# Attention heads of an mLSTM layer: scores of two heads issued together, in three PSUM phases

## The chip, the cores and the metric

One NeuronCore of one Trainium2 chip runs one inference step of a two-layer trunk in float32. The metric is the device time of one execution in microseconds (us), the median over runs. Everything below is about a single core, so no core waits for another.

## What is computed

The trunk has two layers. Layer 0 mixes tokens with an mLSTM (8 heads, keys of 64, values of 128), layer 1 with an S5 state-space model; each is followed by a squared-ReLU MLP. There are 512 prompt tokens in one sequence and 8 sample sequences of 8 tokens, so 576 columns in all. What the change touches is the mLSTM of layer 0, and the final RMSNorm. Cut to that:

```python
for each head h (q, k of width 64, v of width 128, gates i and f):
    logD[t, s] = b[t] - b[s] + li[s]          # s <= t, b is the cumulative sum of log f
    m_t  = max(b[t] + m0, max_s logD[t, s])   # running stabiliser
    s    = (q @ k.T) * 64**-0.5 * exp(logD - m_t)
    num  = exp(b + m0 - m_t) * (q @ C0) + s @ v
    den  = exp(b + m0 - m_t) * (q @ n0) + sum(s)
    h_t  = num / max(|den|, exp(-m_t))
    C1   = decay * C0 + sum_s ws * k v        # new matrix state, and n1 alike
out = (h * rsqrt(mean(h*h) + eps) * head_g * sigmoid(o)) @ w_out
...
y = x * rsqrt(mean(x*x) + eps) * g            # final norm
```

## The kernel before

Activations lie as features by tokens: 128 partitions by 576 columns. Large products are made by `product` (L384) as three products of halves of split float32 numbers. Before the attention stage stands the projection into q, k, v, o; behind it the output projection (`product` with `I_OUT`, weights brought by `load_slab`), then the MLP.

Each engine runs its own list, in program order, and semaphores tie the lists together. In the attention stage each of the lists of TensorE, VectorE, ScalarE and GpSimd has a loop `for h in range(H + 1)` in which work of head h and of head h-1 is interleaved by hand. For head h:

- SyncE sends a row of u to all partitions (`load_u_row`, L510), two buffers, and the matrix state of the sample sequences (`load_state`, L527); it stores the new state (L542, L546) after `c_new`.
- ScalarE makes `exps(h)` (L1017), the decay weights of 512 + 384 + 256 + 128 columns, into `E[:, h % 2]`.
- TensorE makes `scores(h)` (L1910, L1912): q and k of one head lie on 64 partitions, heads 2i on partitions 0 to 63 and heads 2i+1 on 64 to 127. The result fills PSUM banks 1 to 3.
- VectorE multiplies scores and exponentials in `weights(h)` (L1449 over 1280 columns, L1450 for the samples), which signals `p_done`; GpSimd zeroes the upper triangle in `mask(h)` (L745) and signals `p_masked`.
- TensorE makes `sums(h)`: ten products of weights and values (L1935), one of the samples (L1936), and four with the old state `Cst` (L1940), then `pv_done`. The first three sums lie in bank 4, the rest in bank 5.
- ScalarE copies the sums out (L1042, L1043) and scales the state part into `Is` (L1044), signalling `ot_act`. VectorE adds it in (L1526, `ot_ready`).
- TensorE's `updates_b(h)` (L1946, L1963) waits for `ot_act`, since it writes bank 4; `updates_a(h)` follows after the next scores. GpSimd's `keys(h)` (L777 to L781) prepares both, and `sample_queries(h)` (L763) the products with `Cst`.
- VectorE runs `states_b` (L1470 on), `head_norm` (L1497 to L1503), `states_a` (L1456, `c_new`), `normed` (L1508, L1509, `htok_ready`); between them ScalarE makes the squares (L1033) and GpSimd a power (L796).
- TensorE transposes the normed head in `heads_out` (L1921, L1922); VectorE gates it (L1479, L1480), ScalarE casts it (L1022), VectorE makes the low half `hid_lo` (L1485).

TensorE's order in step h is: `updates_b(h-1)`, `scores(h+1)`, `updates_a(h-1)`, `sums(h)`, `heads_out(h-1)`. `weights(h+1)` reads the three banks that `scores(h+2)` will write, so `scores` waits for `p_done`.

Ahead of the loop TensorE transposes keys and values (L1896, L1897), makes the argument of the samples' exponent (L1968), and `scores(0)`; ScalarE makes the samples' exponent (L1025) and then `exps(0)`; GpSimd masks it (L756).

At the very end the sums of squares for the final norm are made by 27 products with `ones` (L2210), over `acc`, `tbuf` and `R`, the last of which needs the last square.

## Time and profile before

| | us |
|---|---|
| median of 3 runs | 1359.15 |
| lowest and highest | 1357.31, 1359.29 |
| profiled execution | 1361.22 |
| its span | 1359.5 |
| TensorE busy | 1306.1 (96%) |
| VectorE busy | 789.5 (58%) |
| ScalarE busy | 491.0 (36%) |
| GpSimd busy | 356.1 (26%) |

The mean granted clock of TensorE is 0.977 of full speed. The attention stage lies between about 201 and 297 us of the span. Times in the rows are microseconds from the start of the span; PE is TensorE's matmul, PEld its weight load, DVE VectorE, ACT ScalarE, POOL GpSimd, SPq SyncE's DMA queue. A float32 product shows as two instructions, a transpose as one.

### The profile page before, as it was taken

How to read it: one execution, taken by the hardware profiler on the slowest of the kernel's cores; microseconds unless marked ns; L12 is line 12 of the kernel's file. 1: busy time of each engine (PE TensorE's matmuls, PEld its weight loads, DVE VectorE, ACT ScalarE, POOL GpSimd, SP SyncE). 2: the span in 40 equal slices, each digit the busy share in tenths (PEclk: the TensorE clock that was granted, in tenths of full speed). 3: DMA queues.
4: the chain of work that ended last, by engine and by line, in shares of the span. 5: the costliest groups of instructions: out<-in, count | busy, mean ns of one | idle time of the engine just before them, and what ended most of it. 6: DMA issues, size and time to landing. Idle time of an engine off the chain costs nothing.

```text
span 1359.5 us, 24599 instructions
## 1 busy us (share of the span) xinstructions
PE 1306.1 (96%) x9929; PEld 1264.0 (93%) x9929; DVE 789.5 (58%) x1102; ACT 491.0 (36%) x743; POOL 356.1 (26%) x360
## 2 busy tenths in 40 slices
PE   4999998999999999999999889999999999999997
PEld 3999996789999999999999878999999999999997
DVE  6662334766783583343345557334588586686785
ACT  5311133543341341341341224423453452543553
POOL 3000004535799990000018553022000000000001
PEclk9999997999999999999999877999999999999999
DMA  5232231324323223223224995233223313223222
GB/s 149 63 91 81 77 95 45 90 59 89 90 78 93 78 77 93 77 81 88 77 78 127 161 133 135 75 91 106 80 77 94 93 62 104 82 94 94 80 75 70
DMA packets 223039, 121.81 MB, mean 90 GB/s; under 512 B 34752, under 2 KB 218744, under 8 KB 222976
## 3 DMA queue, kind: packets, MB, share of 16 engines
q1 hardware_dynamic: 222144, 120.74, 34.7%
q8 instruction: 42, 0.69, 0.2%
q10 hardware_dynamic: 832, 0.21, 0.1%
q14 instruction: 21, 0.17, 0.0%
HBM read 110.18 MB, written 10.75 MB: 89 GB/s over the span
## 4 chain that ended last, share of the span: by engine, by line
PE 84%; DVE 8%; SPq 2%; ACT 2%; issue 2%; DMA 1%; POOL 0%; ACTq 0%; DVEq 0%; POOLq 0%
PE ps L384 62%; PE ps L2131 12%; PE ps L1935 2%; DVE wlo L368 2%; PE ps L1910 1%; PE ps L2087 1%; PE ps L2083 1%; SPq L645 1%; DMA late<-d_taps 1%; SPq L626 1%; PE ps L1946 1%; PE ps L1940 1%; DVE R L405 1%; PE ps L1963 1%; DVE x L1634 1%
## 5 line engine op out<-in xcount | busy, mean ns | idle before, releaser
L384 PE MATMUL ps<-xg_hi,whi 128*128 128x288 f32 x1424 | 305.8, 296 | 3.2 <-DVE wlo L368 1.7
L384 PE MATMUL ps<-xg_hi,wlo 128*128 128x288 f32 x1424 | 304.4, 295 | 0.0
L384 PE MATMUL ps<-xg_lo,whi 128*128 128x288 f32 x1424 | 303.1, 294 | 0.0
L363 ACT ACTIVATE whi<-raw 128x1024 fp32r<-128x1024 f32 x115 | 121.5, 1058 | 352.7 <-PE ps L384 336.0
L384 PEld LDWEIGHTS ps<-xg_hi,whi 128*128 128x128 f32 x1424 | 228.2, 188 | 5.6 <-issue 2.3
L384 PEld LDWEIGHTS ps<-xg_lo,whi 128*128 128x128 f32 x1424 | 228.0, 188 | 0.0
L384 PEld LDWEIGHTS ps<-xg_hi,wlo 128*128 128x128 f32 x1424 | 227.5, 188 | 0.0
L368 DVE TENSOR_TENSOR wlo<-raw,whi 128x1024 fp32r<-128x1024 f32 x115 | 170.9, 1486 | 76.0 <-ACT whi L363 75.9
L384 PE MATMUL ps<-hid_hi,whi 128*128 128x288 f32 x896 | 192.4, 296 | 2.4 <-DVE hid_lo L1779 2.1
L384 PE MATMUL ps<-hid_lo,whi 128*128 128x288 f32 x896 | 192.2, 296 | 0.0
L384 PE MATMUL ps<-hid_hi,wlo 128*128 128x288 f32 x896 | 191.5, 294 | 0.0
L384 PEld LDWEIGHTS ps<-hid_hi,whi 128*128 128x128 f32 x896 | 143.6, 189 | 3.9 <-DVE hid_lo L1779 2.8
L384 PEld LDWEIGHTS ps<-hid_hi,wlo 128*128 128x128 f32 x896 | 144.0, 189 | 0.0
L384 PEld LDWEIGHTS ps<-hid_lo,whi 128*128 128x128 f32 x896 | 143.6, 188 | 0.0
L1535 DVE TENSOR_TENSOR x<-x,ps 128x576 f32 (+1 forms) x40 | 30.2, 754 | 124.9 <-PE ps L384 124.9
L925 POOL TENSOR_TENSOR acc<-hB 128x576 f32<-128x576 f32 x1 | 1.8, 1774 | 350.8 <-ACT hB L1156 350.8
L2131 PE MATMUL ps<-hB_hi,whi 128*128 128x288 f32 x256 | 76.0, 297 | 0.6 <-DVE x L1634 0.6
L2131 PE MATMUL ps<-hB_hi,wlo 128*128 128x288 f32 x256 | 75.4, 295 | 0.0
L2131 PE MATMUL ps<-hB_lo,whi 128*128 128x288 f32 x256 | 75.4, 294 | 0.0
L1553 DVE TENSOR_TENSOR tbuf<-rbuf,R 128x576 f32<-128x576 f32 x32 | 35.7, 1116 | 68.1 <-ACT rbuf L1060 68.0
L1634 DVE TENSOR_TENSOR x<-x,ps 128x288 f32<-128x288 f32 x112 | 50.3, 451 | 32.4 <-PE ps L2131 31.9
L1327 DVE TENSOR_TENSOR qkvo<-ps,R 128x576 f32 (+1 forms) x25 | 18.9, 756 | 77.4 <-PE ps L384 77.3
(397 smaller groups left out, 2083.3 us busy)
## 6 DMA issues: line engine op xcount, KB each, us to landing
raw<-in_ffn_w_up SPq DMA_DIRECT2D x64, 512.0 KB, 4.0
raw<-in_ffn_w_down SPq DMA_DIRECT2D x32, 512.0 KB, 4.2
raw<-in_ffn_w_down SPq DMA_DIRECT2D x16, 1024.0 KB, 5.2
raw<-in_mlstm_w_in SPq DMA_DIRECT2D x25, 512.0 KB, 3.8
raw<-in_s_w_glu SPq DMA_DIRECT2D x16, 512.0 KB, 3.9
raw<-in_mlstm_w_out SPq DMA_DIRECT2D x8, 512.0 KB, 4.2
late<-d_taps SPq DMA_DIRECT2D x32, 128.0 KB, 8.0
d_u<-unat SPq DMA_DIRECT2D x8, 288.0 KB, 2.4
```

Of the source, the lines that this page charges most:

```text
L363: nc.scalar.activation(whi[:, s], raw[:, s], ACT.Copy).then_inc(whi_done, 1)
L368: nc.vector.tensor_tensor(wlo[:, s], raw[:, s], whi[:, s].bitcast(F32), ALU.subtract).then_inc(w_ready, 1)
L384: last = nc.tensor.matmul(ps[:, 2 * s + c, 0:HN], w[:, s, k, :], a[:, k, c * HN:(c + 1) * HN], start=(k == 0 and n == 0), stop=(k == KT - ...
L405: nc.vector.reciprocal(R[:], R[:]).then_inc(R_ready, 1)
L626: sp.dma_start(U2[i * GC:(i + 1) * GC, g, :], d_u.rearrange("(g c) t b -> t c g b", c=GC)[T - 1 - i, :, g]).then_inc(u2_in[half], 16)
L645: sp.dma_start(taps_pair[j][i * GC:(i + 1) * GC], d_taps[2 * j * P:(2 * j + 2) * P, i * GC:i * GC + P].rearrange("(g c) m -> c g m", c=GC) ...
L1327: V.tensor_tensor(halves(tile(qkvo, t)), slab_ps(s), halves(R[:]), ALU.mult).then_inc(ps_free[s], 1)
L1535: V.tensor_tensor(halves(tile(x, m)), halves(tile(x, m)), slab_ps(s), ALU.add).then_inc(ps_free[s], 1)
L1553: V.tensor_tensor(tbuf[:], rbuf[:], R[:], ALU.mult).then_inc(scaled, 1)
L1634: V.tensor_tensor(xh, xh, ps[:, bank, 0:HN], op).then_inc(x_added, 1)
L1935: nc.tensor.matmul(o, e[:, c:c + P], Vtok[:, 1 + j, h, :], start=(j == 0), stop=(j == i))
L2131: last = nc.tensor.matmul(out, w[wi][:, k, :], hi[:, k, t, :], start=(first and k == 0 and n == 0), stop=(k == 3 and n == 2), skip_group_c ...
```

## The change

- Scores are made for a pair of heads (2i, 2i+1) in three phases: banks 0 and 1 take the first 512 columns of both heads, banks 2 and 3 the next 512 (384 + 128), and the last 256 and the samples go to banks 0 and 1 again (banks 6 and 7 for the first pair). Within a phase the products alternate between the two heads, so between partitions 0 to 63 and 64 to 127. Phases 1 and 2 of the next pair are issued in each odd step, phase 3 within `sums`.
- `weights` becomes three instructions, `weights_1`, `_2`, `_3`, of 512, 512 and 256 columns. `weights_1` of both heads of a pair stands ahead of `states_a` in odd steps.
- `E` gets a third buffer; ScalarE makes exponentials two heads ahead. `exps(0)` goes ahead of the samples' exponent, `exps(1)` behind it.
- `keys(0)` goes ahead of the mask of the samples' exponent; in the loop `keys` goes ahead of `mask` and waits for `updates_a` where it waited for `updates_b`; `mask(0)` goes ahead of `sample_queries(0)`.
- After three of the four prompt sums TensorE signals `pv3_done`; ScalarE copies them then (`ot3_act`), and `updates_b` waits for that copy alone.
- `heads_out(h-1)` moves from behind `sums(h)` into it, ahead of the four products with `Cst`.
- 24 transposes of `ident` into bank 5, whose result nobody reads, follow the first pair's scores.
- SyncE sends rows of u for heads 2 and 3 before the loop, and that of head h+4 between the store and the load of the state.
- The final sums run over `acc` first, then `tbuf`, then `R`, each over all columns, with the waits in front of each.

```diff
@@ -208,8 +208,8 @@
-        E = qkvo[:, 16 - KT:16, :].rearrange("p a n -> p (a n)")[:, 0:2688].rearrange("p (s n) -> p s n", s=2)
-        Es = qkvo[0:TS, 16 - KT:16, :].rearrange("p a n -> p (a n)")[:, 2688:2688 + H * TS]
+        E = qkvo[:, 16 - KT:16, :].rearrange("p a n -> p (a n)")[:, 0:4032].rearrange("p (s n) -> p s n", s=3)
+        Es = qkvo[0:TS, 16 - KT:16, :].rearrange("p a n -> p (a n)")[:, 4032:4032 + H * TS]
...
@@ -529,18 +529,20 @@
 
             load_state(0)
             load_state(1)
+            load_u_row(2)
+            load_u_row(3)
             sp.wait_ge(m_ready, 1)
             with nc.allow_non_contiguous_dma(reason="72 numbers"):
                 sp.dma_start(s_m[0].rearrange("b h -> h b"), gs[:, MPT:MPT + B]).then_inc(out_done, 16)
                 sp.dma_start(p_m[0].rearrange("b h -> h b"), gs[:, MPT + B:MPT + B + 1]).then_inc(out_done, 16)
             for h in range(H):
                 s = h % 2
-                if h + 2 < H:
-                    load_u_row(h + 2)
                 sp.wait_ge(c_new, h + 1)
                 for b2 in range(2):
                     sp.dma_start(s_C[0, b2::2, h].rearrange("b d e -> d b e"),
                                  Cst[b2 * DK:(b2 + 1) * DK, s, :, 0:DV]).then_inc(c_out[s], 16)
+                if h + 4 < H:
+                    load_u_row(h + 4)
                 if h + 2 < H:
                     load_state(h + 2)
                 sp.dma_start(p_C[0, 0, h], CP[:, s, :]).then_inc(c_out[s], 16)
...
@@ -751,11 +753,30 @@
+            def keys(h):
+
+                s = h % 2
+                if h >= 2:
+                    pool.wait_ge(upa_done, h - 1)
+                kc = slice(h % 2 * DK, (h % 2 + 1) * DK)
+                own.link(nc.gpsimd.tensor_tensor(Kws[0:TS, s, 0, :], Ktok[0:TS, 0, h // 2, kc],
+                                                 EX[0:TS, 0, h:h + 1].to_broadcast([TS, DK]), ALU.mult))
+                own.link(nc.gpsimd.tensor_tensor(Kws[:, s, 1:5, :], Ktok[:, 1:5, h // 2, kc],
+                                                 EX[:, 1:5, h:h + 1].to_broadcast([P, NB, DK]), ALU.mult))
+                nc.gpsimd.tensor_tensor(Kblk[:, s], Kws[0:TS, s, 0, :].unsqueeze(1).to_broadcast([TS, B, DK]),
+                                        MB[:].unsqueeze(2).to_broadcast([TS, B, DK]), ALU.mult).then_inc(kws_ready, 1)
+
+            pool.wait_ge(ex_ready, 2)
+            own.link(nc.gpsimd.tensor_scalar(EX[:, :, 0:H], EX[:, :, 0:H], DK ** -0.5, None, ALU.mult))
+            pool.wait_ge(kv_act, 6)
+            pool.wait_ge(kv_dve, 6)
+            keys(0)
             pool.wait_ge(us_exp, 1)
             es = Es.rearrange("s (h t) -> s h t", h=H)
             nc.gpsimd.tensor_tensor(es, es, Msk[:].unsqueeze(1).to_broadcast([TS, H, TS]), ALU.mult).then_inc(es_ready, 1)
             def sample_queries(h):
 
+                pool.wait_ge(p_masked, h + 1)
                 if h:
                     pool.wait_ge(pv_done, h)
                 hp = h % 2 * DK
@@ -768,35 +789,17 @@
                 last.then_inc(qblk_ready, 1)
                 pool.wait_ge(qblk_ready, h + 1)
 
...
-            def keys(h):
-
-                s = h % 2
-                if h >= 2:
-                    pool.wait_ge(upb_done, h - 1)
...
-            pool.wait_ge(ex_ready, 2)
-            own.link(nc.gpsimd.tensor_scalar(EX[:, :, 0:H], EX[:, :, 0:H], DK ** -0.5, None, ALU.mult))
-            pool.wait_ge(kv_act, 6)
-            pool.wait_ge(kv_dve, 6)
-            keys(0)
+
+            mask(0)
             sample_queries(0)
             n_column(0)
-            mask(0)
             for h in range(H + 1):
                 if h:
                     pool.wait_ge(ms_ready, h)
                     nc.gpsimd.tensor_tensor(st5[:, 5, :], st5[:, 4, :], st5[:, 6, :], ALU.pow).then_inc(rstd_ready, 1)
                 if h + 1 < H:
+                    keys(h + 1)
                     mask(h + 1)
-                    keys(h + 1)
                     sample_queries(h + 1)
                     n_column(h + 1)
             square_sums(pool, 1)
...
@@ -1008,10 +1011,10 @@
 
             def exps(h):
 
-                e = E[:, h % 2]
+                e = E[:, h % 3]
                 act.wait_ge(ub_in[h % 2], 16 * (h // 2 + 1))
-                if h >= 2:
-                    act.wait_ge(pv_done, h - 1)
+                if h >= 3:
+                    act.wait_ge(pv_done, h - 2)
                 for j in range(NB):
                     w = L - j * P
                     last = nc.scalar.activation(e[:, OFF[j]:OFF[j] + w], Ub[h % 2][:, j * P:L], ACT.Exp, bias=TK[:, 1 + j, h:h + 1])
@@ -1021,9 +1024,11 @@
                 act.wait_ge(hf_ready, h + 1)
                 nc.scalar.activation(hid_hi[:, h], qkvo[:, 16 + h], ACT.Copy).then_inc(hhi_done, 1)
 
+            act.wait_ge(kv_done, 12)
+            exps(0)
             act.wait_ge(us_arg, 2)
             nc.scalar.activation(Es, Es, ACT.Exp).then_inc(us_exp, 1)
-            exps(0)
+            exps(1)
             for h in range(H + 1):
                 if h:
                     act.wait_ge(ot_ready, h)
@@ -1032,14 +1037,16 @@
                     for i in range(5):
                         last = nc.scalar.activation(Htok[:, i, :], OT[:, i, 0:DV], ACT.Square, accum_out=st5[:, 2, i:i + 1])
                     last.then_inc(ssq_done, 1)
-                if h + 1 < H:
-                    exps(h + 1)
+                if h + 2 < H:
+                    exps(h + 2)
                 if h < H:
 
-                    act.wait_ge(pv_done, h + 1)
+                    act.wait_ge(pv3_done, h + 1)
                     if h:
                         act.wait_ge(htok_ready, h)
-                    nc.scalar.activation(OT[:, 1:4, :], ps[:, 4, 0:3 * E1].rearrange("p (i c) -> p i c", i=3), ACT.Copy)
+                    nc.scalar.activation(OT[:, 1:4, :], ps[:, 4, 0:3 * E1].rearrange("p (i c) -> p i c", i=3),
+                                         ACT.Copy).then_inc(ot3_act, 1)
+                    act.wait_ge(pv_done, h + 1)
                     nc.scalar.activation(OT[:, 4, :], ps[:, 5, 0:E1], ACT.Copy)
                     nc.scalar.activation(Is[:], ps[0:TS, 5, 2 * E1:3 * E1], ACT.Copy, scale=EX[0:TS, 0, 64 + h:65 + h]).then_inc(ot_act, 1)
                 if h:
...
@@ -1440,14 +1447,26 @@
             dve.wait_ge(att_const, 1)
             own.link(V.memset(st5[:, 6, :], -0.5))
 
-            def weights(h):
-
-                e = E[:, h % 2]
+            def weights_1(h):
+
                 dve.wait_ge(exp_done, h + 1)
-                dve.wait_ge(s_done, h + 1)
-                flat = ps[:].rearrange("p b c -> p (b c)")
-                V.scalar_tensor_tensor(e[:, 0:1280], flat[:, 512:1792], DK ** -0.5, e[:, 0:1280], ALU.mult, ALU.mult)
-                V.scalar_tensor_tensor(e[0:TS, 1280:1344], flat[0:TS, 1792:1856], DK ** -0.5, Es[:, h * TS:(h + 1) * TS],
+                dve.wait_ge(s_done, h // 2 * 3 + 1)
+                e = E[:, h % 3, 0:512]
+                V.scalar_tensor_tensor(e, ps[:, h % 2, :], DK ** -0.5, e, ALU.mult, ALU.mult).then_inc(p1_done, 1)
+
+            def weights_2(h):
+
+                dve.wait_ge(s_done, h // 2 * 3 + 2)
+                e = E[:, h % 3, 512:1024]
+                V.scalar_tensor_tensor(e, ps[:, 2 + h % 2, :], DK ** -0.5, e, ALU.mult, ALU.mult)
+
+            def weights_3(h):
+
+                dve.wait_ge(s_done, h // 2 * 3 + 3)
+                e = E[:, h % 3]
+                b = h % 2 + (6 if h < 2 else 0)
+                V.scalar_tensor_tensor(e[:, 1024:1280], ps[:, b, 0:256], DK ** -0.5, e[:, 1024:1280], ALU.mult, ALU.mult)
+                V.scalar_tensor_tensor(e[0:TS, 1280:1344], ps[0:TS, b, 256:320], DK ** -0.5, Es[:, h * TS:(h + 1) * TS],
                                        ALU.mult, ALU.mult).then_inc(p_done, 1)
...
@@ -1490,8 +1509,11 @@
                             TK[0:TS, 0, 0:H].unsqueeze(2).to_broadcast([TS, H, TS]), ALU.add).then_inc(us_arg, 1)
             dve.wait_ge(us_arg, 1)
             V.tensor_scalar(Es, Es, 0.0, None, ALU.min).then_inc(us_arg, 1)
+            weights_1(0)
+            weights_2(0)
             dve.wait_ge(es_ready, 1)
-            weights(0)
+            weights_3(0)
+            weights_1(1)
             def head_norm(h):
 
                 own.link(V.scalar_tensor_tensor(st5[:, 0, :], OT[:, :, DV], -1.0, OT[:, :, DV], ALU.mult, ALU.max))
@@ -1514,11 +1536,15 @@
                 if h:
                     states_b(h - 1)
                     head_norm(h - 1)
+                if h % 2 and h + 1 < H:
+                    weights_1(h + 1)
+                    weights_1(h + 2)
+                if h:
                     states_a(h - 1)
-                if h:
                     normed(h - 1)
                 if h + 1 < H:
-                    weights(h + 1)
+                    weights_2(h + 1)
+                    weights_3(h + 1)
                 if h:
                     gated(h - 1)
                 if h < H:
@@ -1899,17 +1925,27 @@
             pe.wait_ge(kv_dve, 6)
             pe.wait_ge(att_const, 2)
 
-            def scores(h):
-
-                if h:
-                    pe.wait_ge(p_done, h)
-                hp = h % 2 * DK
-                q, k = qkvo[hp:hp + DK, h // 2], qkvo[hp:hp + DK, 4 + h // 2]
-                for j, (b, c) in enumerate(((1, 0), (2, 0), (3, 0), (2, 384))):
+            def scores(i, phase):
+
+                if phase == 1 and i:
+                    pe.wait_ge(p_done, 2 * i)
+                elif phase == 3 and i:
+                    pe.wait_ge(p1_done, 2 * i + 2)
+                elif phase == 3:
+                    pe.wait_ge(us_arg, 1)
+                q, k = qkvo[:, i], qkvo[:, 4 + i]
+                third = 0 if i else 6
+                for j, b, c in {1: ((0, 0, 0),), 2: ((1, 2, 0), (3, 2, 384)), 3: ((2, third, 0),)}[phase]:
                     w = L - j * P
-                    nc.tensor.matmul(ps[:, b, c:c + w], k[:, TS + j * P:TS + (j + 1) * P], q[:, TS + j * P:N],
-                                     start=True, stop=True)
-                nc.tensor.matmul(ps[0:TS, 3, 256:320], k[:, 0:TS], q[:, 0:TS], start=True, stop=True).then_inc(s_done, 1)
+                    for a in range(2):
+                        hp = slice(a * DK, (a + 1) * DK)
+                        last = nc.tensor.matmul(ps[:, b + a, c:c + w], k[hp, TS + j * P:TS + (j + 1) * P], q[hp, TS + j * P:N],
+                                                start=True, stop=True)
+                if phase == 3:
+                    for a in range(2):
+                        hp = slice(a * DK, (a + 1) * DK)
+                        last = nc.tensor.matmul(ps[0:TS, third + a, 256:320], k[hp, 0:TS], q[hp, 0:TS], start=True, stop=True)
+                last.then_inc(s_done, 1)
 
...
             def sums(h):
 
-                e = E[:, h % 2]
+                e = E[:, h % 3]
                 pe.wait_ge(p_masked, h + 1)
                 if h:
                     pe.wait_ge(ot_ready, h)
@@ -1932,8 +1968,14 @@
                     o = ps[:, 4, i * E1:(i + 1) * E1] if i < 3 else ps[:, 5, 0:E1]
                     for j in range(i + 1):
                         c = OFF[j] + (i - j) * P
-                        nc.tensor.matmul(o, e[:, c:c + P], Vtok[:, 1 + j, h, :], start=(j == 0), stop=(j == i))
+                        last = nc.tensor.matmul(o, e[:, c:c + P], Vtok[:, 1 + j, h, :], start=(j == 0), stop=(j == i))
+                    if i == 2:
+                        last.then_inc(pv3_done, 1)
                 nc.tensor.matmul(ps[0:TS, 5, E1:2 * E1], e[0:TS, 1280:1344], Vtok[0:TS, 0, h, :], start=True, stop=True)
+                if h % 2 and h + 1 < H:
+                    scores(h // 2 + 1, 3)
+                if h:
+                    heads_out(h - 1)
                 pe.wait_ge(qblk_ready, h + 1)
                 pe.wait_ge(ncol_ready, h + 1)
                 for b4 in range(4):
...
@@ -1956,7 +1998,7 @@
 
             def updates_b(h):
 
-                pe.wait_ge(ot_act, h + 1)
+                pe.wait_ge(ot3_act, h + 1)
                 pe.wait_ge(kws_ready, h + 1)
                 key_values(h, 3, ps[:, 4, 0:E1])
                 for j in range(NB):
@@ -1968,14 +2010,17 @@
                 last = nc.tensor.matmul(ps[0:TS, 7, h * TS:(h + 1) * TS], SEL[:, h, 0:TS], qkvo[0:8, 24, 0:TS],
                                         start=True, stop=True)
             last.then_inc(us_done, 1)
-            scores(0)
-            pe.wait_ge(us_arg, 1)
-
+            for phase in (1, 2, 3):
+                scores(0, phase)
+
+            for _ in range(24):
+                nc.tensor.transpose(ps[:, 5, 0:P], ident[:], ident[:])
             for h in range(H + 1):
                 if h:
                     updates_b(h - 1)
-                if h + 1 < H:
-                    scores(h + 1)
+                if h % 2 and h + 1 < H:
+                    scores(h // 2 + 1, 1)
+                    scores(h // 2 + 1, 2)
                 if h:
                     updates_a(h - 1)
                 if h < H:
@@ -1983,7 +2028,6 @@
                 else:
                     pe.wait_ge(p_done, H)
                     product(pe, I_OUT, 0, hid, (hid_ready, 0), range(KT - 1))
-                if h:
                     heads_out(h - 1)
             product(pe, I_OUT + 1, 0, hid, None, range(4))
             pe.wait_ge(c_new, H)
@@ -2202,13 +2246,15 @@
             for i in range(2):
                 turn(i, range(6))
             pe.wait_ge(acc_done, ACC0[5])
-            pe.wait_ge(sq0_done, 14)
-            pe.wait_ge(sq7_done, 2)
-            for c in range(0, N, 64):
-                hf, i = (0, 0) if c == 0 else ((c - TS) // 64 % 2, 1 + (c - TS) // P)
-                for a in (acc, tbuf, R):
+            for a in (acc, tbuf, R):
+                if a is tbuf:
+                    pe.wait_ge(sq0_done, 14)
+                elif a is R:
+                    pe.wait_ge(sq7_done, 2)
+                for c in range(0, N, 64):
+                    hf, i = (0, 0) if c == 0 else ((c - TS) // 64 % 2, 1 + (c - TS) // P)
                     last = nc.tensor.matmul(ps[hf * 64:(hf + 1) * 64, 4, 2 * i:2 * i + 2], a[:, c:c + 64], ones[:, 0:2],
-                                            start=(a is acc), stop=(a is R))
+                                            start=(a is acc and c in (0, P)), stop=(a is R), skip_group_check=True)
             last.then_inc(fin_pe, 1)
             for i in range(2):
                 turn(i, range(6, KT)).then_inc(yt_done, 1)
```

## Rows read from the trace of the kernel before

**Rows 1.** Busy time by stretch: stretch, length, each engine's busy us, granted clock, DMA.

```profile
205.00:208.00 3.00, 2.78 (x26) 2.51 (x24) 2.37 (x7) 2.24 (x6) 2.53 (x4) 1.00 1.02 227
208.00:211.40 3.40, 2.60 (x20) 1.86 (x21) 1.81 (x5) 0.24 (x2) 0.00 (x0) 1.00 0.03 6
211.40:225.05 13.65, 11.54 (x38) 8.48 (x36) 3.23 (x4) 4.03 (x9) 7.65 (x19) 0.50 0.07 20
...
240.00:260.00 20.00, 19.59 (x125) 15.07 (x124) 14.86 (x47) 10.22 (x38) 10.48 (x24) 1.00 0.31 86
```

**Rows 2.** The chain of waits in the heads: start, length, what.

```profile
256.84 0.49 PE ps L1946 x2
...
258.35 2.35 PE ps L1910 x8
...
260.96 0.86 PE ps L1946 x6
261.82 2.43 PE ps L1935 x20
...
264.61 1.04 PE ps L1940 x8
...
266.34 0.25 ACT Is L1044
...
266.63 0.49 PE ps L1946 x2
...
285.22 0.59 PE ps L1921 x4
...
294.39 0.49 PE ps L1946 x2
```

**Rows 3.** Timeline of VectorE within one head: start, length, line, operation, idle before.

```profile
248.72 1.08 DVE L1485 TENSOR_TENSOR hid_lo<-qkvo,hid_hi 128x576 fp32r<-128x576 f32 x1 [0.63 <-ACT hid_hi L1022]
249.72 0.27 DVE L1470 COPY CP<-ps 64x128 f32<-64x128 f32 x1
...
252.07 0.87 DVE L1456 SCALAR_TENSOR_TENSOR Cst<-Cst,dcy,ps 128x129 f32<-128x129 f32 x3 [0.64 <-PE ps L1946]
...
253.24 0.83 DVE L1509 TENSOR_TENSOR Htok<-OT,st 128x640 f32<-128x640 f32 x1
254.15 1.49 DVE L1449 SCALAR_TENSOR_TENSOR qkvo<-ps,qkvo 128x1280 f32<-128x1280 f32 x1
...
256.76 0.75 DVE L1479 SCALAR_TENSOR_TENSOR qkvo<-ps,vec,qkvo 128x512 f32<-128x512 f32 x1 [0.99 <-PE ps L1922]
```

**Rows 4.** Timeline of GpSimd in the same head.

```profile
251.50 1.17 POOL L796 TENSOR_TENSOR st<-st 128x5 f32<-128x5 f32 x1 [1.01 <-DVE st L1503]
```

**Rows 5.** Timeline of the start of the stage, weight loads left out.

```profile
209.84 3.12 PE L1910 MATMUL ps<-qkvo 64*128 64x512 f32 x8
...
211.72 1.91 ACT L1017 ACTIVATE qkvo<-acc,TK 128x512 f32<-128x512 f32 x4
211.89 1.26 POOL L756 TENSOR_TENSOR qkvo<-qkvo,Msk 64x512 f32<-64x512 f32 x1 [4.37 <-ACT qkvo L1025]
...
215.47 4.60 PE L1910 MATMUL ps<-qkvo 64*128 64x512 f32 x8 [2.11 <-DVE qkvo L1450]
...
216.24 1.03 POOL L745 TENSOR_SCALAR_AFFINE_SELECT qkvo<-qkvo 128x128 f32<-128x128 f32 x4
...
226.51 0.49 ACT L1042 ACTIVATE OT<-ps 128x387 f32<-128x387 f32 x1 [11.07 <-PE ps L1940]
```

**Rows 6.** S5 stage: timeline of two lines, then instructions of a third by line.

```profile
779.16 0.64 PE L2083 MATMUL ps<-U,late 128*128 128x72 f32 x4 [1.22 <-DMA late<-d_taps]
...
779.73 0.67 PE L2087 MATMUL ps<-Hst,CA 64*128 64x72 f32 x8
...
L2007 PE MATMUL ps<-CA,bblk x128: 272/273/298, 728.1 to 731.6; 128*32 128x128 f32 x128
```

**Rows 7.** Timeline of the final norm.

```profile
1349.12 0.26 ACT L1278 ACTIVATE fin<-ps,eps 64x1 f32<-64x1 f32 x1 [2.19 <-PE ps L2210]
```

40 lines of the change are left out of this document (20 added, 20 removed).

## The prediction

> **What bounds the kernel now.** I read the table by stretch first [rows 1]. From 240 to 260 us, inside the attention heads, TensorE is busy 19.59 of 20 us, VectorE 14.86, ScalarE and GpSimd about half. So the attention stage is TensorE's, and VectorE stands 5 us behind it. The table shows a second thing: from 211.40 to 225.05 TensorE ran at a granted clock of 0.50 (1.2 GHz), ahead of it and in the later heads at 1.00 (2.4 GHz). From 208 to 211.40, before it fell, it was busy 2.60 us, on eight-row products and the first head's scores, which use 64 of its 128 rows.
>
> Then the chain of waits for one head [rows 2]. One period is 256.84 to 266.63, 9.79 us. `updates_b` takes 258.35-256.84 = 1.51, `scores` 260.96-258.35 = 2.61, `updates_a` 0.86, the products over prompt and sample tokens 264.61-261.82 = 2.79, the four `Cst` products 1.04. What is left, 266.63-265.65 = 0.98, holds ScalarE's three copies, which end with `Is` at 266.34+0.25, 0.94 after the last product; under them TensorE does the transposes of `heads_out` (0.59 for four, so about 0.8 for all five) and then waits. VectorE [rows 3] and GpSimd [rows 4] give the parts of the second chain, and the start of the stage [rows 5] gives the serial part: the first exponentials wait for the sample exponent (211.72), the second scores wait 2.11 us for the first weights (215.47), and head 0 is only summed at 226.51.
>
> The profiled execution took 1361.22 us, its span 1359.5; the median shown is 1359.15, 2.07 under the profiled one. I work out differences on the span and take them from the median.
>
> **Scores in pairs.** Two heads lie on array rows 0 to 63 and 64 to 127, and the products now alternate between the halves. Serial, a pair costs 2 x 2.61 = 5.22. Whether halves run side by side is told by another place [rows 6]: with 72 columns, four full-height instructions took 779.73-779.16 = 0.57, 143 ns each, and eight half-height ones that alternate between the halves started within 0.59, 74 ns each; and 128 instructions on four alternating column groups of 128 columns started from 728.1 to 731.6, 27 ns each, which is less than 128 columns need one after the other. So I take the pair at 2.6, bounds 2.6 and 5.2. These two rows have short products and the scores have 512 columns, so the upper end stays for the range.
>
> The Trainium skill (TensorEngine Tiling (Array Packing), Key Properties) says that different tiles run in parallel, and TensorE: Matmul & The Clock Gate (Measured speedup vs the span model) gives 3.07 times for four row tiles at 512 columns, not 4. By that efficiency of 0.77 a pair would be 5.2/1.54 = 3.4, an estimate; the 74 against 143 ns of the trace is nearer to a full factor.
>
> **VectorE's weights.** One instruction over 1280 elements (1.49) becomes three, of 512, 512 and 256. The 512-wide one next to it takes 0.75 [rows 3], so (1.49-0.75)/768 is 0.96 ns an element, and 256 cost about 0.50. 0.75+0.75+0.50 = 2.0, so 0.5 more a head, some of it overlapped from one instruction to the next. It is not TensorE's time, but it lies in VectorE's chain: before an odd step two `weights_1` (1.4 together) stand ahead of `states_a`, and `states_a` and `normed` wait behind them.
>
> **The period after.** `updates_b` waits only for the copy of the first three sums, which is over before the last sum, so the wait of about 0.2 goes. TensorE's own sum is 1.51+0.86+2.79+0.81+1.04 = 7.0 without scores, and 7.0+2.6 = 9.6 with a pair. But `heads_out` now stands ahead of the four `Cst` products, and these, with the copies behind them, end the head. So a second chain has to be added up, from the end of the copy `Is` of head h, called t. ScalarE casts the head before and VectorE's `hid_lo` begins at about t+0.8 (an estimate: the row shows 0.63 idle for that cast, plus issue); it takes 249.72-248.72 = 1.00 [rows 3]; `states_b` and the norm's small instructions last to GpSimd's power, 251.50-249.72 = 1.78, so t+3.6; the power takes 1.17 [rows 4], t+4.8. In a step without `weights_1` the product `Htok` follows at t+5.05 and takes 0.83: t+5.9. With them: 3.6+1.4, `states_a` up to the product 253.24-252.07 = 1.17, product 0.83: t+7.0. Then transposes 0.81, `Cst` 1.04, and ScalarE's last two copies (the 0.94 less most of the first one's 0.49), 0.6: t+8.4 and t+9.5; I take 8.5 and 9.6. So where scores stand TensorE and VectorE's chain end together, and where they don't VectorE's chain sets the time and TensorE idles some 1.5 us. In all seven periods after head 0: three with a pair (steps 1, 3, 5) and four without, 3 x 9.6 + 4 x 8.5 = 62.8. Step 1 has no earlier head to gate, 0.5 less: 62.3. Before: six periods of 9.79 and a last one without scores; `updates_b` of head 7 starts at 294.39, 286.21 is three periods after 256.84, so the last is 8.18: 66.9. Saving 4.6. At the end of the stage `updates_b` starts 0.5 earlier: 5.1.
>
> **The front.** Today head 0's copies start at 226.51, so `Is` ends at 226.51+0.9 = 227.4 [rows 2, 5]. After: `exps(0)` no longer waits for the sample exponent and runs from about 208 to 210 (1.91), while ScalarE is idle now (0.24 of 3.40 busy, GpSimd 0.00) [rows 1, 5]. The sample exponent still ends at 211.7, GpSimd's mask of it (211.89, 1.26) ends at 213.15, as now, since `keys(0)` lies in GpSimd's idle time before. `weights_1` and `weights_2` of head 0 are done by then; `weights_3`, 0.50 and the sample part of about 0.2, ends at 213.9, GpSimd's `mask(0)` (1.03 at 216.24 today) 1.1 later, 215.0. TensorE: paired scores of heads 0 and 1 from 209.84 to 212.4, then 24 transposes. Such transposes cost 2.78/26 = 107 ns [rows 1], 2.6 in all, to 215.0. They are hidden by the wait for the mask; without that cover they cost 2.6. `sums(0)` from 215.1, 2.79+1.04, copies 0.6: 219.6 [rows 2, 5]. That is 7.8 sooner. It needs the full clock. What speaks for it: from 205 to 208, when the code gives TensorE only such transposes, the clock stayed at 1.00; and of 208 to 211.4 the part with scores now uses both halves.
>
> The Trainium skill (TensorE: Matmul & The Clock Gate, Part 4: PE-mode transpose) says that transposes do not count as activity for the clock. By that the 24 would not hold it; the row of 205 to 208 speaks against that, though it shows a clock kept, not one regained.
>
> **The rest.** Rows of u are sent two heads ahead: ScalarE's exponentials are not last today, so nothing. In the final norm the sums of `acc` and `tbuf` go ahead of those that need the last square. ScalarE waits 2.19 there, for the products by `ones` [rows 7]; bounds 0 and about half of it, I take 0.2. All later stages shift as they are. GpSimd now makes `keys` ahead of `mask`: it is busy about 5.2 a head, of which 1.17 and 1.03 are power and mask, so keys and the rest are at most 3.0 [rows 1, 4, 5] and end by t+7.8, about when `weights_3` does; the mask is wanted at t+10.6 or later, so nothing. `load_u_row(2)` and `(3)` stand before the output of the maxima, which nobody waits for.
>
> Sum: 7.8 + 5.1 + 0.2 = 13.1, so 1359.15 - 13.1 = 1346.
>
> **Rivals.**
> (a) *The clock falls in the front all the same.* It speaks for it that it falls there today. At half clock the rest of the paired scores costs about 1 more, the 24 transposes 2.6 more, and 1.5 to 3 us of `sums(0)` the same again, in part beside the waits for VectorE: 3 to 6 in all. 1349 to 1352. It is also where the rule on transposes leads.
> (b) *The chains are longer than added up, or the halves overlap only in part.* A pair of 3.4 costs 0.8 in each of three steps and about 1 in front; a power, a DMA of the state or an exponential that comes late by 0.5 in each step costs 3.5. 1348 to 1354.
> (c) *Slower: the two heads' scores do not run side by side.* Then the change does not do what it says. With a pair at 5.2 the odd step is TensorE's, 7.0+5.2 = 12.2 against 9.6: 3 x 12.2 + 4 x 8.5 = 70.6, 3.7 longer than the 66.9 of today. In the front the pair then works one half at a time, as today where the clock fell: 1.56 us of it before 211.4, the other 3.7 at half clock to 218.7, the transposes at half clock 5.2 to 223.9, `sums(0)` 3.8, copies: 228.3, 0.9 later than today. Less 0.7 for the end of the stage and the norm: 1363. It decides above a pair of about 4.9. The 74 ns of [rows 6] speak against it.
> (d) *The clock falls inside the stage*, because TensorE now idles 1.5 of 8.5 us. From 240 to 260 the full clock goes with 0.4 us idle in 20; no row chosen here shows it kept with as much idle time as the new short steps have, and 2.60 of 3.40 busy on half-height work lost it. A spell like today's, 13.65 us at half clock, would hold back up to half of that in TensorE's work, 4 to 7 with the waits it covers; the chance is small, the price 4 for one and up to 30 for several: 1350 to 1375.
>
> **How the numbers follow.** Forecast 0.48 (1346, its own range 1343 to 1349), (a) 0.22, (b) 0.20, (c) 0.05, (d) 0.05. Low end 1343: the 24 transposes or the chain turn out shorter by a few tenths in each step. High end 1354, which takes in (a) and (b); (c) and most of (d) are left out. Faster and slower mean by over 0.2%, 2.7 us, about what a measurement of this kernel can tell from no change. Faster: forecast, (a), (b) and a fifth of (d), 0.91, less 0.01 for (b) at its worst: 0.90. Slower: (c) and most of (d), 0.07, and 0.03 lie within.
>
> **What would show it.** Right: granted clock 1.00 from 205 to 240; `sums(0)` starts near 215; a pair's scores last 2.6 to 3 us in two pieces; steps of 8.5 and 9.6 in turn; in the short step TensorE waits before `heads_out` for VectorE's `Htok`; the output products after head 7 start some 13 us sooner. Wrong: 0.50 anywhere after 211 (a, d); pieces of the paired scores of 3.7 and 1.4 us (c); TensorE waiting for ScalarE, for the state's DMA or for GpSimd (b).

## The result, and the profile after

The changed kernel takes 1347.38 us (median of 4 runs, 1345.91 to 1349.74) against 1358.48 for the kernel before in the same comparison: a ratio of 0.9908, 95% interval 0.9889 to 0.9926. Forecast was 1346, range 1343 to 1354. The profiled execution took 1348.39, its span 1346.6, which is 12.9 less than the span before. The medians in the same comparison differ by 11.1, where 13.1 had been forecast.

First the table by stretch as in [rows 1], of the kernel after: stretch, length, busy time of PE, PEld, DVE, ACT and POOL, granted clock, DMA.

```profile
208.00:211.79 3.79, 2.77 (x28) 1.87 (x28) 2.24 (x7) 2.46 (x6) 2.38 (x5) 1.00 0.19 40
211.79:215.20 3.41, 3.41 (x21) 2.35 (x18) 2.21 (x6) 3.28 (x7) 1.46 (x2) 0.50 0.18 61
215.20:225.00 9.80, 9.80 (x79) 8.27 (x77) 3.81 (x15) 4.95 (x19) 5.48 (x18) 1.00 0.14 29
...
240.00:260.00 20.00, 18.42 (x135) 14.10 (x135) 16.39 (x52) 11.52 (x48) 10.15 (x23) 1.00 0.41 96
```

Three things differ. ScalarE and GpSimd work from 208 on, where they stood nearly idle. The stretch at half clock is 3.41 us and not 13.65. And in the heads TensorE is busy 18.42 of 20 us, not 19.59, with VectorE up from 14.86 to 16.39: VectorE's chain now comes last in some steps.

Then the start of the stage, which answers [rows 5]: start, length, engine, line, operation, idle before.

```profile
208.56 1.91 ACT L1020 ACTIVATE qkvo<-acc,TK 128x512 f32<-128x512 f32 x4
209.43 1.11 PE L2010 MATMUL ps<-qkvo,SEL 8*64 8x64 f32 x16 [1.02 <-ACT Vtok L1010]
210.47 3.38 PE L1942 MATMUL ps<-qkvo 64*128 64x512 f32 x16
212.63 1.26 POOL L776 TENSOR_TENSOR qkvo<-qkvo,Msk 64x512 f32<-64x512 f32 x1 [1.03 <-ACT qkvo L1030]
...
214.19 3.31 PE L2017 MATMUL ps<-ident 128*128 128x128 f32 x24
...
215.00 1.03 POOL L747 TENSOR_SCALAR_AFFINE_SELECT qkvo<-qkvo 128x128 f32<-128x128 f32 x4 [1.11 <-DVE qkvo L1469]
...
217.34 2.40 PE L1971 MATMUL ps<-Vtok,qkvo 128*128 128x129 f32 x20
```

The first exponentials (L1020) run before the samples' exponent, head 0 is masked at 216.03, and its sums begin at 217.34. They don't wait for the mask, which is 1.31 us old by then, but for TensorE's own 24 transposes (214.19 to 217.34), of which the first part ran at half clock, as did most of the scores ahead of them (3.38 us).

Then TensorE in two steps, a long one with a pair's scores and a short one, which answers the chain of [rows 2].

```profile
221.47 1.09 PE L2005 MATMUL ps<-Vtok,Kws 128*64 128x129 f32 x8
222.50 2.00 PE L1942 MATMUL ps<-qkvo 64*128 64x512 f32 x12
224.32 0.83 PE L1988 MATMUL ps<-Vtok,Kblk 64*128 64x129 f32 x6
225.09 2.50 PE L1971 MATMUL ps<-Vtok,qkvo 128*128 128x129 f32 x20
227.51 0.43 PE L1974 MATMUL ps<-Vtok,qkvo 64*64 64x129 f32 x2
227.88 0.70 PE L1942 MATMUL ps<-qkvo 64*128 64x256 f32 x4
228.51 0.33 PE L1947 MATMUL ps<-qkvo 64*64 64x64 f32 x4
228.77 0.66 PE L1957 MATMUL ps<-ident,Htok 128*128 128x128 f32 x4
229.36 0.27 PE L1958 MATMUL ps<-ident,Htok 64*128 64x64 f32 x1
229.56 1.10 PE L1982 MATMUL ps<-Cst,Qblk 128*64 128x129 f32 x8
230.59 0.49 PE L1988 MATMUL ps<-Vtok,Kblk 64*128 64x129 f32 x2
...
235.71 0.43 PE L1974 MATMUL ps<-Vtok,qkvo 64*64 64x129 f32 x2
237.19 0.66 PE L1957 MATMUL ps<-ident,Htok 128*128 128x128 f32 x4 [1.04 <-DVE Htok L1531]
237.97 1.10 PE L1982 MATMUL ps<-Cst,Qblk 128*64 128x129 f32 x8
239.00 0.49 PE L1988 MATMUL ps<-Vtok,Kblk 64*128 64x129 f32 x2
```

Phases 1 and 2 of a pair's scores last 224.32-222.50 = 1.82, phase 3 with the samples 228.77-227.88 = 0.89: 2.71 for two heads, where [rows 2] show 2.61 for one. The updates start right behind the `Cst` products, with no wait. By the first updates of each head (L1988, at 221.06, which is not shown, 230.59 and 239.00) the first step here is 9.53 and the second 8.41. In the first no line has a wait: it is TensorE's own work from end to end. In the short step TensorE waits 1.04 for `Htok` (L1531), the product that VectorE makes last, and 0.35 for VectorE's `Cst` (L1475), so 1.39 in all. The waits of TensorE from 222 to 285, in the heads, are these two and no others: line, released by, us in total, times, longest.

```profile
PE ps L1957 <- DVE Htok L1531: 3.4, 5, 1.0
PE ps L1971 <- DVE Cst L1475: 1.4, 4, 0.4
```

Before, it waited for ScalarE's copies, 0.20 in each head after the first [rows 2].

Where the 12.9 us of span went, from the same points in both traces:

| | before | after | less by |
|---|---|---|---|
| start of the stage (first product for the samples' exponent) | 208.80 | 209.43 | -0.63 |
| from there to the first product of the output projection | 87.90 | 75.45 | 12.45 |
| of it: from the start to the updates of head 0 | 19.08 | 12.04 | 7.04 |
| of it: seven steps from updates to updates, and 1.89 behind the last | 68.82 | 63.41 | 5.41 |
| final norm, transposes to square root [rows 7] | 3.65 | 3.37 | 0.28 |
| all other stages | | | 0.8 |

(A step is taken here and below from the updates by `Kws`, L2005 after and L1963 before, to the next, which can differ by 0.01 from the steps above.) The first line and the last are no work of the change: the start lies ahead of it, and the 0.8 comes from the stages between, above all the S5 stage (about 755 to 850), where TensorE falls to half clock for stretches that differ from execution to execution. Over the whole span these sum to 64.7 us in the execution before and 54.9 in the one after, and to between 32.6 and 72.1 in the experiments. So below an effect of one or two us is read from the length of the attention stage, and the totals stand beside it. Each length is that of one profiled execution.

### The profile page after: what moved, and what is told of

Read it like the earlier page. It is cut to its first block, busy times and chain, and to the rows that moved or that the text cites. A ratio compares the mean times of both kernels' runs of the same rounds, so it can differ in the third digit from the quotient of the medians.

```text
span 1346.6 us, 24669 instructions
## 1 busy us (share of the span) xinstructions
PE 1295.8 (96%) x9953; PEld 1258.2 (93%) x9953; DVE 791.3 (59%) x1118; ACT 490.5 (36%) x743; POOL 355.4 (26%) x360
## 4 chain that ended last, share of the span: by engine, by line
PE 81%; DVE 9%; SPq 3%; DMA 2%; ACT 2%; issue 2%; POOL 1%; ACTq 0%; DVEq 0%; POOLq 0%
PE ps L384 63%; PE ps L2175 12%; DVE wlo L368 1%; PE ps L2131 1%; SPq L628 1%; PE ps L2127 1%; DMA late<-d_taps 1%; SPq L647 1%; DMA Cst<-in_state_mlstm_C 1%; DMA out<-Cst 1%; DVE R L405 1%; DVE x L1660 1%; PE ps L1942 0%; DVE xg_lo L436 0%; DVE hid_lo L1583 0%
```

## The experiments

Each is an edit of the kernel after. "First sums" is the time from the start of the stage to `sums(0)`; the steps run from updates to updates. A ratio is to the kernel before, run in the same comparison. The unchanged kernel after stands beside e10 and e11 (as e9), but not beside e1 to e8, and from one comparison to the other the ratio of nearly the same kernel differs: 0.986 for e5 and 0.9909 for e10. So totals are set against each other only within e1 to e4, e5 to e8 or e9 to e11. The whole table first, so that each can be set beside the others:

| | first sums | steps | stage | half clock in the stage |
|---|---|---|---|---|
| before | 11.61 | 9.79 x6, 8.18 | 87.90 | 13.65 |
| after | 7.91 | 9.53 8.42 9.83 8.37 9.53 7.97 7.87 | 75.45 | 3.41 |
| e1 one half | 13.51 | 11.79 7.95 11.79 7.95 11.79 7.95 7.87 | 86.62 | 10.24 |
| e2 no transposes | 6.19 | 9.53 8.47 9.84 7.94 9.53 8.06 7.87 | 75.12 | 3.41, later |
| e3 12 transposes | 6.62 | 9.53 8.39 9.83 8.35 9.84 7.95 7.93 | 74.57 | 3.41 |
| e4 `heads_out` last | 6.34 | 9.40 7.95 9.46 8.30 9.47 7.94 8.19 | 73.06 | none |
| e5 n column late | 6.33 | 9.70 7.95 9.77 7.94 9.77 7.94 7.93 | 73.36 | none |
| e6 updates wait for all | 6.34 | 10.22 8.21 10.22 8.21 10.22 9.32 8.12 | 77.57 | none |
| e7 old front | 7.93 | 9.53 9.37 10.41 7.95 10.07 10.54 10.32 | 82.25 | 3.41, 3.41, 10.24 |
| e8 three edits | 6.21 | 9.40 7.94 9.40 7.95 9.64 7.94 7.95 | 72.54 | none |
| e9 unchanged | 6.34 | 9.53 8.50 9.83 7.95 10.10 7.97 7.95 | 74.20 | none |
| e10 n column late | 7.91 | 9.72 7.96 9.97 7.95 9.79 7.95 7.94 | 75.20 | 3.41 |
| e11 n column, `heads_out` | 7.91 | 9.39 7.95 9.39 7.96 9.64 7.95 7.94 | 74.16 | 3.41 |

**e1: both heads' scores from the same half.** The count, size and order of all instructions stay; only the halves are gone, and with them the scores of the odd heads: the kernel computes those of the even head twice. The same edit is made in the samples' scores of phase 3.

```diff
                     for a in range(2):
-                        hp = slice(a * DK, (a + 1) * DK)
+                        hp = slice(0, DK)
```

> The kernel after the change, but both heads of a pair take their q and k from partitions 0 to 63, so nothing alternates between halves of the array (the scores of odd heads are thereby those of the head before, all shapes and counts stay). Theory, halves run side by side: a pair then costs about 5.2 us instead of 1.82+0.89, the odd steps of 9.5 to 9.8 become TensorE's with 12, so 7 to 8 us more in the three odd steps, and 2.5 to 6 in the front: 1357 to 1361 against 1347, and the granted clock is at 0.50 for longer. Rival, the halves don't matter and the pair is short for another reason (order, fewer waits): pair 2.7, time unchanged.

Measured: 1358.26, ratio 0.998 (0.9965 to 0.9996): the gain is nearly gone, and the 2.7 us that are left are what all the other edits are worth without the halves. TensorE in the first long step:

```profile
227.41 3.71 PE L1942 MATMUL ps<-qkvo 64*128 64x512 f32 x12
230.97 0.83 PE L1988 MATMUL ps<-Vtok,Kblk 64*128 64x129 f32 x6
...
234.52 1.13 PE L1942 MATMUL ps<-qkvo 64*128 64x256 f32 x4
235.57 0.44 PE L1947 MATMUL ps<-qkvo 64*64 64x64 f32 x4
235.95 0.66 PE L1957 MATMUL ps<-ident,Htok 128*128 128x128 f32 x4
```

The twelve instructions last 3.56 and not 1.82, the pair 3.56 + 1.43 = 4.99 and not 2.71. So the two halves do work side by side, 1.84 times as fast as one after the other. The long step becomes 11.79. The front shows the other half of the matter, in e1's table by stretch and in its transposes:

```profile
208.00:211.38 3.38, 2.64 (x20) 1.86 (x21) 1.85 (x5) 1.92 (x5) 1.94 (x3) 1.00 0.13 41
211.38:221.62 10.24, 10.24 (x36) 7.63 (x35) 3.59 (x8) 4.09 (x9) 4.04 (x11) 0.50 0.13 42
221.62:225.00 3.38, 3.38 (x30) 3.08 (x29) 0.00 (x0) 0.49 (x1) 1.78 (x5) 1.00 0.02 5
```

```profile
217.67 4.74 PE L2017 MATMUL ps<-ident 128*128 128x128 f32 x24
```

From 211.38 on the clock is at half for 10.24 us, against 3.41 at most in the front of the eleven executions that use both halves. That the halves set this length rests on one execution of e1 and one of the kernel before (13.65). The stage is 11.2 longer than after: 5.6 of it lie ahead of the first sums (13.51 against 7.91) and 5.6 in the steps (67.1 against 61.5), where three long ones are 2.0 to 2.3 longer and the short ones 0.0 to 0.5 shorter, since VectorE's chain has more time.

**e2 and e3: the transposes.** e2 has none of the 24, e3 has 12.

```diff
-            for _ in range(24):
-                nc.tensor.transpose(ps[:, 5, 0:P], ident[:], ident[:])
```

> The 24 transposes behind the first pair's scores are left out, nothing else. Theory, they keep or regain the clock: without them TensorE idles from about 214 to 216, the granted clock stays at 0.50 well into the sums of heads 0 and 1 and the stage gets 2 to 5 us longer: 1349 to 1352. Rival, they only stand in the way (the mask of head 0 was done 1.3 us before the sums began): sums of head 0 start 1.3 us sooner, the clock is as before, time 1346.

> 12 transposes instead of 24. Theory: they end about when GpSimd's mask of head 0 does, so the sums of head 0 start 1.0 to 1.3 us sooner and the granted clock is what it was: 1346 to 1346.5. Rival: with fewer of them the clock comes back later and the gain is gone or reversed, 1347 to 1350.

Measured: 1347.93, ratio 0.9898 (0.9866 to 0.9931), and 1344.73, ratio 0.9881 (0.9852 to 0.991). In e2 neither the theory (2 to 5 longer) nor the rival (1346) came out: the sums start 1.7 sooner, but the half clock has only moved. TensorE, and the stretches:

```profile
215.05 0.33 PE L1947 MATMUL ps<-qkvo 64*64 64x64 f32 x4
217.84 4.07 PE L1971 MATMUL ps<-Vtok,qkvo 128*128 128x129 f32 x20 [2.46 <-POOL qkvo L747]
```

```profile
213.00:217.73 4.73, 2.38 (x20) 1.19 (x16) 3.95 (x8) 3.59 (x8) 3.05 (x6) 1.00 0.16 55
217.73:221.14 3.41, 3.30 (x15) 3.30 (x16) 0.63 (x3) 0.97 (x3) 3.03 (x9) 0.50 0.25 79
```

TensorE idled 2.46 us, the clock fell at 217.73, at the end of that wait, and the twenty products took 4.07 instead of 2.40. That the idle time made it fall is not shown by this one execution. So without the transposes the 1.7 that the sums gain in starting is lost in their length, and the stage is 75.12 against 75.45. With 12 it is 74.57: the same 3.41 at half clock, and a shorter queue in front of the sums, which start after 6.62 where 24 gave 7.91. Where the clock stays up the number hardly matters: 6.34 with 24 (e9), and 6.21 with 12 (e8), which then wait 1.02 for the mask. So half the number is enough of a cover here. What the 24 are worth against none isn't settled: the stage without them is 0.3 shorter than that of the kernel after and 0.9 longer than that of e9, and these differ by the clock.

**e4: `heads_out(h-1)` behind the `Cst` products again.**

```diff
-                if h:
-                    heads_out(h - 1)
                 pe.wait_ge(qblk_ready, h + 1)
...
-                    heads_out(h - 1)
+                if h:
+                    heads_out(h - 1)
```

> heads_out(h-1) goes back behind the four products with Cst, as before the change. Theory, one chain through VectorE sets the short steps whichever way: the Cst products no longer wait for Htok, but gating and hid_lo then come later by the same amount; steps within 0.4 of 8.4 and 9.6, total within 1.5 us of 1347. Rival, heads_out in front is a new wait that costs: short steps fall to about 7.5, total 1343 to 1344.

Measured: 1342.41, ratio 0.9866 (0.9827 to 0.9905). The stage is 73.06, but this execution had no stretch at half clock in the front. That is chance, as e9 shows, and worth 1.6 (10.48 in e9 from the start to the updates of head 0, against 12.04). Against e9's 74.20, with the same clock, the stage is 1.1 shorter. The long steps say what the place is worth: 9.40, 9.46, 9.47 against 9.53, 9.83, 9.53. So the place behind is better by 0.1 to 0.4 a long step, and e11 against e10, which differ in this alone, have 9.39, 9.39, 9.64 against 9.72, 9.97, 9.79. The short steps did not fall to 7.5, as the rival had it, but two of the four are 7.95 and 7.94.

**e5 and e10: the copy of the n column behind the power.** In the kernel after GpSimd copies it in front of the norm's power, and it waits for the new head's state to land. e5 has the final norm in its old order besides.

```diff
                     sample_queries(h + 1)
-                    n_column(h + 1)
...
                     ..., ALU.pow).then_inc(rstd_ready, 1)
+                    if h < H:
+                        n_column(h)
```

> Two edits that are far apart in time, each read at its own place. First: GpSimd's n_column(h) goes from ahead of the power of the head before to behind it. Theory: in the short steps the power waited about 0.5 us for the state's DMA, which n_column waits for; without that the steps of 8.4 fall to about 7.9, the stage from 75.45 to 74.2 at the same clock. Rival: it is VectorE's chain alone, steps unchanged. Second: the final norm in its old order. Theory: 0.3 us more from its transposes to the square root (3.37 back to 3.65). Both together: within 1 us below 1347.

> n_column(h) behind the power, alone. Theory: short steps all 7.9 to 8.0, none above, no fall of the clock inside the stage: stage 73.4 at full clock in the front, 75 with a spell there; 1 to 3 us below the kernel after in the same call. Rival: in the mean over executions the power's wait is nothing and the two are equal within 0.5.

Measured: 1340.84, ratio 0.986 (0.9837 to 0.9884), and 1346.62, ratio 0.9909 (0.9896 to 0.9923). First the two instructions of GpSimd in the kernel after, then in e10:

```profile
234.68 0.19 POOL L754 COPY Cst<-nT 128x4 f32<-128x4 f32 x1 [3.30 <-DMA Cst<-in_state_mlstm_C]
234.83 1.17 POOL L799 TENSOR_TENSOR st<-st 128x5 f32<-128x5 f32 x1
```

```profile
236.00 1.17 POOL L799 TENSOR_TENSOR st<-st 128x5 f32<-128x5 f32 x1 [3.02 <-DVE st L1526]
237.12 0.19 POOL L754 COPY Cst<-nT 128x4 f32<-128x4 f32 x1
```

After, VectorE had the mean square ready at 234.27 and the power began at 234.83, 0.56 later, behind a copy that waited 3.30 for a DMA. In e10 the power waits for VectorE alone and begins 0.16 after it, so 0.40 of the 0.56 was the copy's. All short steps are 7.94 to 7.96, where after has 8.42, 8.37 and 7.97, and in none of the kernels with this edit (e5, e8, e10, e11) is one above 7.96. But the long steps give some of it back: 9.72, 9.97, 9.79 against 9.53, 9.83, 9.53. The sum of the seven steps is 61.28 against 61.52, and 61.00 in e5 against 61.83 in e9, so this edit partly moves a wait and partly removes it: 0.2 to 0.8 us. By the totals it shows nothing: e10 is equal to e9 (1346.62 and 1346.47), as its rival had it, where 1 to 3 less were expected. That e5's total is 6 lower than e10's is not the old order of the norm (in e5 the transposes start at 1320.30 and the square root at 1323.95, 3.65 as before, against 3.37 after), which can only make it longer. The two stand in different comparisons, e5's runs alone reach from 1336.05 to 1346.14, and its profiled execution had 32.6 us at half clock in all, the least of any. The order of the norm is worth 0.28.

**e6: updates wait for the copy of all sums.**

```diff
-                pe.wait_ge(ot3_act, h + 1)
+                pe.wait_ge(ot_act, h + 1)
```

> updates_b waits again for all of ScalarE's copies (ot_act), not for the first alone. Theory: odd steps are TensorE's and get 0.6 us longer each, short ones are VectorE's and stay; the stage gets 1.8 to 2.5 us longer, 1349. Rival: TensorE never is last and the stage stays at 75.4.

Measured: 1350.59, ratio 0.9903 (0.9874 to 0.9932). The stage is 77.57, against 74.20 in e9, which has the same front in the code and as much clock. The steps are 10.22 and 8.21, but one is 9.32: there the copy of the n column waited 4.24 for its DMA and TensorE 1.65 for `Htok`, which is the chain of e5 and not this edit. The wait for the copies is there in each head:

```profile
250.82 0.49 PE L1988 MATMUL ps<-Vtok,Kblk 64*128 64x129 f32 x2 [0.62 <-ACT Is L1051]
```

So the signal after the first three sums is worth 0.3 to 0.7 a step with this order of the work (8.21 and 10.22 against the 7.95 and 9.53 of undisturbed steps), more than the 0.20 that was waited before: with `heads_out` in front of the `Cst` products nothing covers the copies any more.

**e7: the old order in front.** Exponentials of head 0 behind the samples' exponent, `keys(0)` behind its mask.

```diff
-            exps(0)
             act.wait_ge(us_arg, 2)
             nc.scalar.activation(Es, Es, ACT.Exp).then_inc(us_exp, 1)
+            exps(0)
...
-            keys(0)
             pool.wait_ge(us_exp, 1)
             ...
+            keys(0)
             mask(0)
```

> The front in its old order: ScalarE's first exponentials behind the sample exponent, GpSimd's keys(0) behind the mask of it. Theory: head 0's sums then start about 8.1 us after the stage's first products, against 6.3 at full clock and 7.9 with the cold spell in the profile of after, and the stage is 0.5 to 2 us longer than with the same clock. Rival: the first weights were not last and nothing moves.

Measured: 1344.51 median, ratio 0.9863 (0.9834 to 0.9892), with runs from 1340.01 to 1356.36; the profiled execution is the 1356.36. In front the sums start after 7.93, as in the kernel after: `mask(0)` ends at 218.43, and the sums start at 218.48, behind the transposes, which again ran partly at half clock. So where such a stretch happens, the two moves win nothing. What they win where it doesn't, no run shows; an estimate is the 7.88 us from the start to this mask less the 6.34 of e9, so 1.5. The median gives them no worth either: it is not above that of e8, which was run beside it. The profile showed more by what it had not been made for, in its table by stretch:

```profile
236.67:240.08 3.41, 2.09 (x16) 1.49 (x15) 2.50 (x6) 0.60 (x2) 3.25 (x4) 1.00 0.54 116
240.08:243.49 3.41, 3.41 (x15) 2.55 (x13) 1.59 (x4) 2.50 (x14) 1.56 (x7) 0.50 0.48 129
...
274.22:277.63 3.41, 1.52 (x12) 1.02 (x10) 1.74 (x5) 0.49 (x1) 2.90 (x5) 1.00 0.29 77
277.63:287.87 10.24, 10.24 (x43) 8.98 (x43) 5.89 (x21) 3.05 (x14) 3.73 (x9) 0.50 0.21 53
```

The clock fell twice inside the stage, after stretches in which TensorE was busy 2.09 and 1.52 of 3.41 us. In the first, GpSimd's copy had waited 3.55 for its DMA and TensorE 1.32 for `Htok`. What made TensorE idle before the second fall, on GpSimd and on TensorE:

```profile
274.57 0.19 POOL L754 COPY Cst<-nT 128x4 f32<-128x4 f32 x1 [4.13 <-DMA Cst<-in_state_mlstm_C]
274.73 1.16 POOL L799 TENSOR_TENSOR st<-st 128x5 f32<-128x5 f32 x1
```

```profile
277.08 0.66 PE L1957 MATMUL ps<-ident,Htok 128*128 128x128 f32 x4 [1.89 <-DVE Htok L1531]
```

A state that landed late held the copy, the copy the power, the power VectorE's product and this the transposes, 1.89 us; then the steps took 10.54 and 10.32. The trace shows no way from the front's edit to this, which lies 20 to 60 us later; the chain through the n column stands in the kernel after as well. That the idle time made the clock fall is argued from the order of the two, not tried by itself.

**e8, e9, e11: together, and the kernel after again.** e8 is e3, e4 and e10 in one, e11 is e4 and e10, e9 has no edit and was run beside them, more often.

> After the change, with three edits together: 12 transposes, n_column behind the power, heads_out behind the Cst products. Theory: the sums of head 0 at 6.3 us, long steps of 9.4, short ones of 7.9, stage about 72.5: 1341 to 1344. Rival: once one wait is gone the next one takes its place, stage 73 to 74 as with the single edits, 1343 to 1345.

> The kernel after the change once more, on the chip and in the call of the next two, so that they stand beside it. Theory: in the steps without scores the power waits behind n_column for the state's DMA, by 0.3 to 2 us; long steps 9.5 to 9.8, short ones 8.0 to 8.5 with one above 9 possible; where TensorE idles long there the granted clock can fall inside the stage. Stage 73.5 to 77, total 1344 to 1350. Rival: the waits of the profiled execution are typical and every step repeats to 0.1.

> n_column(h) behind the power and heads_out behind the Cst products, 24 transposes kept. Theory: long steps 9.4, short ones 7.95, so about 1 us less than n_column alone in the stage (72.5). Rival: equal to n_column alone within 0.3.

Measured: e8 1344.92, ratio 0.988 (0.9861 to 0.99); e9 1346.47, ratio 0.9917 (0.9896 to 0.9938); e11 1345.53, ratio 0.9907 (0.9893 to 0.9921). e9's profiled execution had no half clock in the front:

```profile
210.38 2.43 PE L1942 MATMUL ps<-qkvo 64*128 64x512 f32 x16
213.00 2.84 PE L2017 MATMUL ps<-ident 128*128 128x128 f32 x24
215.67 2.40 PE L1971 MATMUL ps<-Vtok,qkvo 128*128 128x129 f32 x20
```

The same code, with scores of 2.43 and not 3.38 and transposes of 2.84 and not 3.31, has its first sums 1.6 sooner. Of the seven executions with this front (after, e4, e5, e6, e9, e10, e11) three had the stretch of 3.41 us and four had none. e8 has the shortest stage, 72.54, 1.7 less than e9 with the same clock, as expected, and all its short steps are 7.94 or 7.95. e11's is 74.16 with the stretch at half clock, 1.0 less than e10's with the same, also as expected. The totals don't tell e8, e10 or e11 from the kernel after: the intervals overlap, and the S5 stage's clock moves a total by more than that. e9's steps (8.50 and 7.95 for short ones, 10.10 for a long one) rule out its rival, that every step repeats to 0.1.

## Why the prediction was right, and where it was off

- **The pair of scores**, taken at 2.6 with bounds 2.6 and 5.2: 2.71. e1 shows 4.99 with one half. The choice of the short products of [rows 6] over the upper bound held for 512 columns as well. The Trainium skill (TensorE: Matmul & The Clock Gate, Measured speedup vs the span model) would by its efficiency of four row tiles have given 3.4, an estimate; two halves measured 1.84, 0.92 of a full factor.
- **Rival (c)** is out by e1, and e1 also shows that it was priced too high: 2.7 below the kernel before, not 4 above it (1363). The long step came to 11.79 where 12.2 had been worked out, and the short ones to 7.95 where 8.5 had been, 0.4 and 0.5 too much in each. In front, e1 reaches the updates of head 0 1.4 sooner than before (17.65 against 19.08), where 0.9 later had been worked out.
- **The long step**, 9.6: 9.53, 9.83, 9.53. The forecast took 0.5 off the first of them, since no earlier head is gated there. That was wrong: this step is TensorE's own work without a wait, and a shorter chain on VectorE takes nothing off it.
- **The short step**, 8.5: 8.42, 8.37, 7.97, and the last step of all 7.87. The seven sum to 61.52; forecast 62.3, so the short ones came out 1.4 shorter together and the long ones 0.6 longer. In the first short step `Is` ends at 231.22 and the next one at 239.63, t+8.41, where t+8.4 had been added up: two errors cancel there. `hid_lo` was taken at 1.00 from [rows 3], from t+0.8 on. Before, it took from 0.76 to 1.22 with GpSimd at work beside it; in the changed kernel all eight take 0.76, and GpSimd is idle then (here it waits from 231.38 to 234.68 for the DMA). VectorE in the short step above:

```profile
231.90 0.76 DVE L1504 TENSOR_TENSOR hid_lo<-qkvo,hid_hi 128x576 fp32r<-128x576 f32 x1 [0.35 <-ACT hid_hi L1025]
232.57 0.28 DVE L1489 COPY CP<-ps 64x128 f32<-64x128 f32 x1
...
234.10 0.17 DVE L1525 TENSOR_SCALAR st<-st 128x5 f32<-128x5 f32 x1
...
236.31 0.82 DVE L1531 TENSOR_TENSOR Htok<-OT,st 128x640 f32<-128x640 f32 x1
```

  It starts at t+0.68, and from its start to the next instruction it is 0.67: 0.12 and 0.33 less than taken. So the chain by itself is t+7.95, which is what e10 and e11 have, and the wait behind the copy of the n column, which the forecast's chain did not have, brings it back to 8.4. That wait is the part of **rival (b)** that came true: a DMA of the state is late, but by about 0.4 to 0.5 and in two of the short steps, not in each.
- **VectorE's weights**: three instructions for one, as forecast, and TensorE's waits in the heads name none of them. They take 0.69, 0.68 and 0.41 in the mean of the eight heads, 1.78 together, so 0.3 more than the one of 1.49, where 0.5 had been forecast. VectorE's busy time, 791.3, is 1.8 above that before.
- **The front**, 7.8, was to come at granted clock 1.00 with the sums near 215. It did not: 0.50 from 211.79 to 215.20, and the sums at 217.34. The measured gain is 7.04 from the start to the updates of head 0. Without the stretch at half clock the first sums start after 6.33 or 6.34 (e4, e5, e6, e9), and 6.3 had been worked out (215.1 less the start at 208.80). With it they start after 7.91. So **rival (a)** did happen in the profiled execution, by the prediction's own sign for it, at 1.6 and not at 3 to 6: half clock lasted 3.41 us and had ended when the sums began. Some 0.9 came back between the sums and the updates, 221.47-217.34 = 4.13, where 4.5 to `Is` and, as before, about 0.5 from there stood in the sum: the updates no longer wait for `Is`. The forecast had put that 0.5 down to the end of the stage, which did not change (1.89 in both).
- **The sum.** For the stage 12.9 were forecast and 12.45 measured, and this is -1.6 for the clock, +0.9 between sums and updates, +0.8 in the steps (5.4 for 4.6) and -0.5 for the end. So the mechanism held, pairs side by side and TensorE relieved until VectorE's chain comes last, but the close agreement is in part luck, in the sum as in the short step. In an execution without the spell the same kernel's stage is 74.20 (e9), 1.3 shorter.
- **Rival (d)** stayed away in the kernel after and in all kernels with its order but came in e7's profiled execution, at 6.8 us (82.25 against 75.45). The prediction gave it 0.05 and no reason for so small a chance. The idle time it counted on in a short step, 1.5, is what the kernel after has (1.39); in e7 a late state came on top, with 1.89 in one wait ahead of the second fall. The two waits had not been added up.
- **The rest**: final norm 0.28, forecast 0.2. The third buffer of `E`, the order of the phases and the rows of u were not tried alone. `weights_1` of head h+2 now stands ahead of `c_new` of head h+1 on VectorE, and the old sending order would make the row wait for that `c_new`; so the move is needed for the order of the work, and no run gives it a time of its own.

## What to carry to other kernels

When products use only half the rows, pair them over the two halves: it bought most of this change's gain, in the time of the products and, as far as one execution of e1 shows, again in the clock at the start of the stage. Once TensorE is relieved, add up the next engine's chain from end to end, small copies and the DMA they wait for among it, and let nothing that waits for a transfer stand ahead of an instruction on that chain. Read effects of one or two us from the stage, not from totals that a later stage's clock moves by more.

## What the runs showed of the chip

- Two 64-row halves at up to 512 columns of float32 ran 1.84 times as fast as one half (2.71 against 4.99 for a pair), also when the two passes of one product stand next to each other in the order.
- The granted clock is not fixed by the code. With the same code in front it went to 0.50 for 3.41 us in three executions and stayed at 1.00 in four. With scores on one half alone it stayed at 0.50 for 10.24 (e1) and 13.65 (before), though in e1 TensorE was busy all that time. The last two are one execution each.
- The clock was kept and regained under float32 transposes alone. In the kernel before it stayed at 1.00 from 201.16 to 207.99, with TensorE busy 6.62 of 6.83 us on transposes of keys and values only. In e1 it came back to 1.00 at 221.62, when TensorE had done nothing but transposes since 217.67. The Trainium skill (TensorE: Matmul & The Clock Gate, Part 4: PE-mode transpose) says that transposes don't count as activity for the clock in the way that products do; these two traces do not agree. The return at 215.20 in the kernel after doesn't decide it, since scores ran until 214.19.
- A VectorE instruction that reads two float32 tiles of 128x576 took up to 1.22 us where GpSimd worked at the same time and 0.76 in all eight cases of the kernel after, where it was idle. Once before it took 0.76 (at 239.30) with GpSimd copying beside it; there GpSimd's copy took 1.01 where it takes 0.47 in the kernel after. That the two hold each other up is argued from the timelines, not tried by itself.
